# PEER gates through DRAM in three sets of 64 tokens in place of one set of 128

## The chip, the cores and the metric

One core of one Trainium2 chip. The metric is the time of the program on the device in microseconds (us), a median over runs.

## What is computed

A trunk of two layers on 256 tokens of width 1024: a short gated convolution (layer 0) or latent attention (layer 1), and after each a PEER channel mixer. The mixer picks, for every token and each of 8 heads, 16 of 16,384 experts, and sums their outputs:

```python
q = (xc @ w_q).reshape(C, PEER_HEADS, 2, PEER_HALF)
s = jnp.einsum("chpd,hpnd->chpn", q, subkeys)
top_s, top_i = lax.top_k(s, PEER_TOPK)
cand = top_s[:, :, 0, :, None] + top_s[:, :, 1, None, :]
best_s, best_pos = lax.top_k(cand.reshape(C, PEER_HEADS, PEER_TOPK * PEER_TOPK), PEER_TOPK)
ia = jnp.take_along_axis(top_i[:, :, 0], best_pos // PEER_TOPK, axis=-1)
ib = jnp.take_along_axis(top_i[:, :, 1], best_pos % PEER_TOPK, axis=-1)
expert = ia * PEER_KEYS + ib
g = jax.nn.softmax(best_s, axis=-1)
act = jax.nn.gelu(jnp.einsum("chkd,cd->chk", u_tab[expert], xc), approximate=False) * g
return jnp.einsum("chk,chkd->cd", act, v_tab[expert])
```

## The kernel before

The kernel does not gather experts. It multiplies all 16,384 u rows with all 256 tokens, takes the gelu, weighs it with a dense grid of gates (zero where an expert was not chosen), and multiplies the result with all v rows. The first key number `ia` has 128 values, which are worked through in four quarters of 32. One panel is the 128 experts of one `ia`: 128 x 1024 f32, 512 KB. A panel is loaded by SP into one of four buffers (`raw`), split by ACT into a rounded high part (`split_hi`, line 1012, four buffers) and by DVE into the remainder (`split_lo`, line 1414, two buffers); POOL splits panels in the stages before, but not in the mix. PE uses both parts. SP may load panel i when the low part of panel i-4 is made (semaphore `panel_lo_ready`).

The stages of one layer's PEER part are `sel` (the choice of the experts), `ahead` (26 u panels, j = 0 to 25), `mix` (three times 64 panels; `mix_body(q, it)`, q = 0 to 2, it = 0 to 7, does 4 u panels for quarter q+1 and 4 v panels for quarter q, u and v in turn), and `last` (32 v panels). The panels of one q are counted here from 0 to 63; panel 40 is the first u panel of `it` 5, panel 41 the v panel behind it. ACT's order around them is `split_hi(40)`, `split_hi(41)`, gelu of panel 36, copy of panel 38's bank, copies of gates, and `split_weighted`, whose result PE needs for panel 41.

The dense gates of a quarter (128 x 32 x 256 f32, in `arena`) must be there before that quarter is weighed. They are made in two ways:

- by matmul: a block is 16 tokens. DVE makes one-hot rows (`hot_b`, `hot_a`, `hot_g`, lines 1631 to 1640), PE multiplies them (`scatter` in the ahead stage, line 704; `scatter_side` in the mix, line 692), ACT and DVE copy the result to `arena` (lines 1083 and 1650). Quarter 1 of the four is made in ahead (16 blocks); in the mix, an `it` run with `by_matmul` makes two blocks of the next quarter.
- by DRAM: for tokens 0 to 127, POOL adds each chosen gate to a grid in DRAM with indirect transfers (`add_gates_by_dma`, line 1389): one transfer for each of the 128 (head, rank) pairs of a layer, 128 gates in each. After the 16 transfers of a head, POOL waits until they have all landed. ACT zeroes the grid (line 1092), and SP reads it into `arena` (`load_grid`, line 422): 8 loads of 4 first keys for each of the last two quarters.

So an `it` with `by_matmul` false is lighter for PE, ACT and DVE. Here all 8 `it` of q = 0 run by matmul; in q = 1 and 2, `it` 0 to 3 are light, and SP issues the grid loads ahead of the panels of `it` 5, 6 and 7 (3, 3 and 2 loads), behind a wait for the last transfer.

PE runs in program order. Its stream is written by hand, as are those of the other engines.

Of the kernel before, what the change touches and what calls it, by code (L numbers as in the profile page):

```python
# [60 lines left out]
BACK = 15  # L61
FIRST = KEYS // 8
BLOCKS = 48
NTH = {0: 16, 1: 24, 2: 32}
BY_GRID = 4
# [50 lines left out]
def program(nc, xT_in, c_in, pos_in, vec_in, con_in, ada_in, pan_in, key_in, iota_in, u_in, v_in, out):  # L116
    ctx = ExitStack()
    grid = [nc.dram_tensor(f"gates_by_expert{l}", (KEYS * KEYS * P, 1), F32, kind="Internal").ap() for l in range(2)]
    with ctx:
# [80 lines left out]
        place = sb("place", [P, SEL], I32)  # L200
        tok = sb("tok", [P, 1])
# [16 lines left out]
        row_start = arena[:, 12032:12032 + SEL]  # L218
        kept = g32_t[:, 0:SEL]
# [20 lines left out]
        GB = ps[6:8]  # L240
        BC = (SC[0], SC[1], STAT, SC[0], SC[1])
# [33 lines left out]
        start_ready = sem("row_starts_ready")  # L275
# [3 lines left out]
        added = [sem(f"gates_of_head{h}_added") for h in range(HEADS)]  # L279
# [97 lines left out]
        def _(sp):  # L377
# [16 lines left out]
            def load_experts(l):  # L394
# [23 lines left out]
                def load_grid(quarter, n):  # L418

                    a = quarter * QUART + 4 * n  # L420
                    to = arena[:, (quarter % 2 * QUART + 4 * n) * T:(quarter % 2 * QUART + 4 * n + 4) * T]
                    sp.dma_start(to.rearrange("p (a t) -> p a t", t=T)[:, :, 0:P],
                                 grid[l][a * KEYS * P:(a + 4) * KEYS * P].rearrange("(a p t) o -> p a (t o)", p=P, t=P)
                                 ).then_inc(s_grid, 16)

                with sp.Fori(0, 8) as it:
                    mix_loads(0, it)
                for q in (1, 2):
                    with sp.Fori(0, BY_GRID) as it:
                        mix_loads(q, it)  # L430
                    mix_loads(q, BY_GRID)
                    if q == 1:
                        sp.wait_ge(added[HEADS - 1], 16 * TOPK * (l + 1))
                    sp.wait_ge(w_mul, 64 * l + 16 * q)
                    for g, parts in enumerate(((0, 1, 2), (3, 4, 5), (6, 7))):
                        for n in parts:
                            load_grid(q + 1, n)
                        mix_loads(q, BY_GRID + 1 + g)
# [57 lines left out]
        def _(pe):  # L496
# [211 lines left out]
            def peer(l):  # L708
# [34 lines left out]
                def turn_back():  # L743

                    pe.wait_ge(idx_copied, TT * (l + 1))
                    for n, numbers in enumerate((ia_t, ib_t)):
                        by_rank = numbers[:, 0:P * DUP].rearrange("p (t r) -> p t r", r=DUP)[:, :, 0]
                        mm = pe.matmul(SC[0][:, n * P:(n + 1) * P], by_rank, ident_b[:], start=True, stop=True)
                    mm.then_inc(back_done, 1)

                for j in range(AHEAD - EARLY):
                    if j in TURN:
                        turn(TURN.index(j))
                    if j == BACK:
                        turn_back()
# [5 lines left out]
                pe.wait_ge(place_ready, l + 1)  # L761
# [13 lines left out]
                with pe.Fori(0, 8) as it:  # L775
                    mix_body(0, it, True)
                for q in (1, 2):
                    with pe.Fori(0, BY_GRID) as it:
# [227 lines left out]
        def _(act):  # L1006
# [84 lines left out]
            def peer(l):  # L1091
                nc.scalar.dma_start(grid[l][2 * QUART * KEYS * P:KEYS * KEYS * P].rearrange("(p c t) o -> p c (t o)", p=P, t=P),
                                    zero[:].bitcast(F32).unsqueeze(1).broadcast_to([P, 2 * QUART, P])).then_inc(s_zero, 16)
# [27 lines left out]
                def row_starts():  # L1121

                    act.wait_ge(tokens_ready, 1)
                    act.wait_ge(back_done, l + 1)
                    nc.scalar.activation(row_start, SC[0][:, P:2 * P], ACT.Identity, bias=tok[:], scale=float(P)
                                         ).then_inc(start_ready, 1)
                    nc.scalar.mul(kept, gate[:, 0, :], G_SCALE).then_inc(gates_kept, 1)
# [79 lines left out]
            act.sem_inc(g_read, 2)  # L1207
            act.wait_ge(s_c, 16)
# [143 lines left out]
        def _(pool):  # L1352
# [17 lines left out]
            pool.iota(tok[:], [[P, 1]], 0, 1, allow_small_or_imprecise_dtypes=True).then_inc(tokens_ready, 1)  # L1370
# [11 lines left out]
            def add_gates_by_dma(l):  # L1382

                pool.wait_ge(s_zero, 16 * (l + 1))
                pool.wait_ge(place_ready, l + 1)
                pool.wait_ge(gates_kept, l + 1)
                for h in range(HEADS):
                    for n in range(h * TOPK, (h + 1) * TOPK):
                        pool.indirect_dma_start(grid[l], bass.IndirectOffsetOnAxis(place[:, n:n + 1], 0), kept[:, n:n + 1], None,  # L1389
# [747 lines left out]
```

## Time and profile before

| | |
|---|---|
| median of 3 runs | 1887.38 us (1886.09 to 1890.06) |
| profiled execution, its own time | 1886.6 us |
| span in its profile | 1884.8 us |
| granted TensorE clock, mean | 0.992 of full speed |
| PE busy | 1866.2 us (99%) |
| DVE busy | 1492.7 us (79%) |
| ACT busy | 1001.2 us (53%) |
| POOL busy | 783.3 us (42%) |
| memory traffic, mean | 206 GB/s |

The profiled execution lies 0.8 us below the median. Of its time 1.8 us lie outside the span. A row of a timeline gives the start in us from the span's start, the duration in us, engine, line, operation and operands; brackets at its end give the idle time before it and who ended it. Layer 0's mix begins at about 301 us of the span, layer 1's at about 1243 us.

### The profile page before, as it was taken

To read this page: it belongs to the slowest core of one execution; us is meant where nothing else is said; L and a number is where in the kernel's file an instruction comes from. 1 tells how busy PE (TensorE), PEld (TensorE's weight loads), DVE (VectorE), ACT (ScalarE), POOL (GpSimd) and SP (SyncE) were. 2 spreads that over 40 slices of the span, in tenths; PEclk is the share of its full clock that TensorE was granted. 3 is DMA by queue.
4 is the path that set the end of the run, shared out by engine and by line. 5 is a ranking of instruction groups with operands and counts; after the bars stand their busy time and mean duration, and the time that the engine had idled before them with its cause. 6 is when DMAs were issued, how large, how long until landed. Compare 5 with 4: busy or idle time off the path is not lost.

```text
span 1884.8 us, 37910 instructions
## 1 busy us (share of the span) xinstructions
PE 1866.2 (99%) x12642; PEld 1655.2 (88%) x12642; DVE 1492.7 (79%) x2893; ACT 1001.2 (53%) x1598; POOL 783.3 (42%) x378
## 2 busy tenths in 40 slices
PE   8999999999999999999999999999999999999999
PEld 7999998888888888887789999988888888888887
DVE  6758999999778977997765489988887678668866
ACT  4354555555555555554454645555555555555553
POOL 3877548788860000000062575487888820000000
PEclk8999999999999999999998999999999999999999
DMA  9986657898897777876632565577777776667664
GB/s 352 364 271 202 187 136 185 229 225 230 229 244 245 257 233 236 264 233 225 223 114 83 170 200 168 136 159 182 184 179 189 190 215 194 187 193 215 190 191 140
DMA packets 174340, 388.82 MB, mean 206 GB/s; under 512 B 48801, under 2 KB 84001, under 8 KB 173857
## 3 DMA queue, kind: packets, MB, share of 16 engines
q1 hardware_dynamic: 120960, 379.01, 64.0%
q0 software_dynamic: 36864, 0.15, 4.7%
q10 hardware_dynamic: 16416, 8.39, 1.6%
q8 instruction: 56, 0.92, 0.2%
q14 instruction: 44, 0.35, 0.1%
HBM read 377.92 MB, written 9.57 MB: 206 GB/s over the span
## 4 chain that ended last, share of the span: by engine, by line
PE 92%; DVE 4%; DMA 2%; ACT 1%; issue 1%; POOL 1%; DVEq 0%; SPq 0%; ACTq 0%; POOLq 0%
PE bank L673 36%; PE bank L658 18%; PE bank L663 9%; PE bank L637 6%; PE bank L642 6%; PE bank L638 6%; PE bank L692 2%; PE bank L704 1%; DMA raw<-in_v_panels 1%; PE bank L720 1%; PE bank L522 1%; PE bank L502 1%; PE bank L953 1%; PE bank L504 1%; PE bank L503 1%
## 5 line engine op out<-in xcount | busy, mean ns | idle before, releaser
L1012 ACT CAST w_hi<-raw 128x1024 fp32r<-128x1024 f32 (+1 forms) x603 | 630.5, 1046 | 327.9 <-PE bank L673 104.0
L1414 DVE TENSOR_TENSOR w_lo<-raw,w_hi 128x1024 fp32r<-128x1024 f32 x488 | 596.9, 1223 | 192.4 <-PE bank L673 88.5
L1389 POOL DMA_INDIRECT gates_by_expert<-g_t,place x256 | 504.9, 1972 | 190.0 <-DVE place L1713 76.4
L1361 POOL TENSOR_TENSOR w_lo<-raw,w_hi 128x1024 fp32r<-128x1024 f32 (+2 forms) x115 | 273.3, 2380 | 528.3 <-PE bank L673 381.4
L658 PE MATMUL bank<-act_two,w_hi 128*128 128x512 f32 x1536 | 379.3, 389 | 0.0
L658 PEld LDWEIGHTS bank<-act_two,w_hi 128*128 128x128 f32 x1536 | 288.3, 188 | 59.8
L673 PE MATMUL bank<-w_hi,wt_hi 128*128 128x512 f32 x1024 | 325.5, 398 | 1.9 <-DVE wt_lo L1676 1.2
L673 PE MATMUL bank<-w_lo,wt_hi 128*128 128x512 f32 x1024 | 317.9, 391 | 0.0
L673 PE MATMUL bank<-w_hi,wt_lo 128*128 128x512 f32 x1024 | 317.0, 390 | 0.0
L637 PE MATMUL bank<-act_two,w_hi 128*128 128x256 f32 x984 | 246.1, 288 | 0.0
L638 PE MATMUL bank<-act_two,w_hi 128*128 128x256 f32 x984 | 241.2, 283 | 0.0
L673 PEld LDWEIGHTS bank<-w_hi,wt_lo 128*128 128x128 f32 x1024 | 192.3, 188 | 41.9
L673 PEld LDWEIGHTS bank<-w_lo,wt_hi 128*128 128x128 f32 x1024 | 192.2, 188 | 41.8
L663 PEld LDWEIGHTS bank<-act_two,w_lo 128*128 128x128 f32 x1536 | 209.5, 190 | 15.0
L663 PE MATMUL bank<-act_two,w_lo 128*128 128x256 f32 x1536 | 213.9, 282 | 0.0
L673 PEld LDWEIGHTS bank<-w_hi,wt_hi 128*128 128x128 f32 x1024 | 178.1, 189 | 32.0 <-issue 4.2
L1065 ACT COPY ring_g<-bank 128x256 f32 (+1 forms) x192 | 71.7, 374 | 253.1 <-PE bank L663 245.1
L638 PEld LDWEIGHTS bank<-act_two,w_hi 128*128 128x128 f32 x984 | 188.5, 192 | 0.0
L637 PEld LDWEIGHTS bank<-act_two,w_hi 128*128 128x128 f32 x984 | 188.2, 191 | 0.0
L642 PE MATMUL bank<-act_two,w_lo 128*128 128x256 f32 x984 | 138.5, 283 | 0.0
L642 PEld LDWEIGHTS bank<-act_two,w_lo 128*128 128x128 f32 x984 | 127.2, 192 | 0.0
L1631 DVE TENSOR_TENSOR hot_b<-ib_t,iota 128x2048 bf16<-128x2048 bf16 x96 | 116.9, 1218 | 0.8 <-PE bank L704 0.8
(257 smaller groups left out, 1951.2 us busy)
## 6 DMA issues: line engine op xcount, KB each, us to landing
raw<-in_u_panels SPq DMA_DIRECT2D x256, 512.0 KB
raw<-in_v_panels SPq DMA_DIRECT2D x256, 512.0 KB
raw<-in_panels SPq DMA_DIRECT2D x81, 512.0 KB
ada<-in_ada_rows SPq DMA_DIRECT2D x56, 512.0 KB
arena<-in_ada_rows SPq DMA_DIRECT2D x40, 512.0 KB, 7.0
gates_by_expert<-zero ACTq DMA_DIRECT2D x2, 4096.0 KB, 22.2
arena<-gates_by_expert SPq DMA_DIRECT2D x32, 256.0 KB, 5.3
gates_by_expert<-g_t,place POOLq DMA_INDIRECT x256
```

The source lines that it names most:

```text
L637: pe.matmul(bank, w_hi[:, hi_slot, w], acts[0][k], start=(k == 0), stop=False)
L638: pe.matmul(bank, w_hi[:, hi_slot, w], acts[1][k], start=False, stop=False)
L642: mm = pe.matmul(bank, w_lo[:, lo_slot, w], acts[0][k], start=False, stop=(k == KB - 1))
L658: pe.matmul(bank[:, 0:2 * T], w_hi[:, hi_slot, w], act_two[:, :, a], start=(k == 0), stop=False, skip_group_check=True)
L663: mm = pe.matmul(bank[:, 0:T], w_lo[:, lo_slot, w], act_hi[:, a], start=False, stop=(k == KB - 1), skip_group_check=True)
L673: mm = pe.matmul(YB[2 * t + n][:], wt[:, par, a], (w_hi, w_lo)[v][:, slots[v], n * 512:(n + 1) * 512], start=False, stop=False, skip_group ...
L1012: nc.scalar.copy(w_hi[:, slot, 0:width], raw[:, slot, 0:width]).then_inc(hi_done, 1)
L1065: nc.scalar.copy(ring_g[:, bass.ds(slot * T, T)], bank[:, T:2 * T]).then_inc(lo_copied, 1)
L1361: pool.tensor_tensor(w_lo[:, lo_slot, 0:width], raw[:, slot, 0:width], w_hi[:, slot, 0:width].bitcast(F32), ALU.subtract).then_inc(lo_done, 1)
L1389: pool.indirect_dma_start(grid[l], bass.IndirectOffsetOnAxis(place[:, n:n + 1], 0), kept[:, n:n + 1], None, compute_op=ALU.add).then_inc(a ...
L1414: dve.tensor_tensor(w_lo[:, lo_slot, 0:width], raw[:, slot, 0:width], w_hi[:, slot, 0:width].bitcast(F32), ALU.subtract).then_inc(lo_done, 1)
L1631: dve.tensor_tensor(wide(hot_b[:, par, :]), each(ib_t, KEYS, token0), numbers(0, KEYS), ALU.is_equal)
```

## The change

The tokens that go through DRAM become three sets of 64: set 0 (tokens 0 to 63) for quarters two to four, set 1 (64 to 127) for quarters three and four, set 2 (128 to 191) for the last quarter. One transfer now holds two ranks of a head for 64 tokens (128 gates again), so a set takes 64 transfers and a layer 192 in place of 128. POOL waits after the 8 transfers of a head and set. The light `it` are 0 and 1 in q = 0, 0 to 3 in q = 1, and 0 to 5 in q = 2: 12 in place of 8 in a layer. The grid is laid out by second key first, and set 2 has a grid of its own. Numbers and gates of a set are turned back by six small matmuls on PE, in ahead at j = 12 (sets 0 and 1) and at j = 15 (set 2). The cut diff:

```diff
-BACK = 15
+BACK = {12: (0, 1), 15: (2,)}
-BLOCKS = 48
-NTH = {0: 16, 1: 24, 2: 32}
-BY_GRID = 4
+SET = 64
+SETS = 3
+BLOCKS = 40
+BY_GRID = (2, 4, 6)
+FETCH_FROM = (5, 6, 5)
...
-                with sp.Fori(0, 8) as it:
-                    mix_loads(0, it)
-                for q in (1, 2):
-                    with sp.Fori(0, BY_GRID) as it:
+                for q in range(3):
+                    first = FETCH_FROM[q]
+                    with sp.Fori(0, first) as it:
                         mix_loads(q, it)
-                    mix_loads(q, BY_GRID)
-                    if q == 1:
-                        sp.wait_ge(added[HEADS - 1], 16 * TOPK * (l + 1))
-                    sp.wait_ge(w_mul, 64 * l + 16 * q)
-                    for g, parts in enumerate(((0, 1, 2), (3, 4, 5), (6, 7))):
-                        for n in parts:
+                    sp.wait_ge(added[q], 16 * SET * (l + 1))
+                    if q:
+                        sp.wait_ge(w_mul, 64 * l + 16 * q)
+                    for it in range(first, 8):
+                        for n in range((it - first) * 8 // (8 - first), (it - first + 1) * 8 // (8 - first)):
                             load_grid(q + 1, n)
-                        mix_loads(q, BY_GRID + 1 + g)
+                        mix_loads(q, it)
...
+                sp.dma_start(to[:, :, 0:tokens], by_key(grid0[l], P)[:, :, 0:tokens]).then_inc(s_grid, 16)
+                    if quarter == 3:
+                        sp.dma_start(to[:, :, P:P + SET], by_key(grid1[l], SET)).then_inc(s_grid, 16)
...
+                for n, grid, w, q in ((0, grid0, P, 1), (1, grid1, SET, 3)):
+                    to = grid[l].rearrange("(p n) o -> p (n o)", p=P)[:, q * QUART * w:KEYS * w]
...
+                for g in range(SETS):
+                    grid = (grid0, grid0, grid1)[g][l]
+                    pool.wait_ge(place_ready, SETS * l + g + 1)
+                    pool.wait_ge(gates_kept, SETS * l + g + 1)
+                    for h in range(HEADS):
+                        for n in range(g * SET + h * TOPK // 2, g * SET + (h + 1) * TOPK // 2):
+                            pool.indirect_dma_start(grid, bass.IndirectOffsetOnAxis(place[:, n:n + 1], 0), kept[:, n:n + 1], None,
+                                                    compute_op=ALU.add).then_inc(added[g], 16)
+                        pool.wait_ge(added[g], 16 * SET * l + 16 * TOPK // 2 * (h + 1))
...
+                def places(g):
+
+                    dve.wait_ge(gates_kept, SETS * l + g + 1)
...
+                for g in BACK[12]:
+                    places(g)
```

SP's queue in q = 0 of layer 0, at the end of `it` 4; before (`raw` are the panel buffers, `ada` a row of modulation weights):

```order
L382 DMA raw<-in_v_panels 128x1024
L406 REGISTER_ALU
L407 ISA [waits ada1_used]
L407 DMA ada<-in_ada_rows 128x1024
L426 REGISTER_ALU
L426 COMPARE_AND_BRANCH
```

and now:

```order
L387 DMA raw<-in_v_panels 128x1024
L411 REGISTER_ALU
L412 ISA [waits ada1_used]
L412 DMA ada<-in_ada_rows 128x1024
L435 REGISTER_ALU
L435 COMPARE_AND_BRANCH
L429 DMA arena<-gates_of_tile_0 128x4x64 [waits gates_of_set0_added]
L429 DMA arena<-gates_of_tile_0 128x4x64
L387 DMA raw<-in_u_panels 128x1024 [waits panel_lo_ready]
L387 DMA raw<-in_v_panels 128x1024 [waits panel_lo_ready]
```

Before, SP loops from `it` 4 straight to the panels of `it` 5. Now the load of panel 40, the first u panel of `it` 5, stands behind a wait for all 64 transfers of set 0 and behind two grid loads.

PE in the ahead stage between panel 11 and panel 12; before, the turn back stood between panels 14 and 15 (`g_t` holds the gates, `ia_t` and `ib_t` the key numbers):

```order
L704 MATMUL bank<-hot_g,hot_b 128x32 [waits gates_copied,one_hots_ready,chosen_experts_repeated]
L704 MATMUL bank<-hot_g,hot_b 128x32 x31
L748 MATMUL bank<-ident_b,ia_t 128x128 [waits chosen_experts_repeated]
L748 MATMUL bank<-ident_b,ib_t 128x128
L637 MATMUL bank<-act_two,w_hi 128x256 [waits panel_hi_ready,bank_read0]
```

and now, between panels 11 and 12:

```order
L647 MATMUL bank<-act_two,w_lo 128x256 x7
L756 MATMUL bank<-ident_b,ia_t 64x64 [waits chosen_experts_repeated]
L756 MATMUL bank<-ident_b,ia_t 64x64
L756 MATMUL bank<-ident_b,ib_t 64x64 x2
L759 MATMUL bank<-con,g_t 64x64 x2
L756 MATMUL bank<-ident_b,ia_t 64x64 [waits chosen_experts_repeated]
L756 MATMUL bank<-ident_b,ia_t 64x64
L756 MATMUL bank<-ident_b,ib_t 64x64 x2
L759 MATMUL bank<-con,g_t 64x64 x2
L642 MATMUL bank<-act_two,w_hi 128x256 [waits panel_hi_ready,bank_read0]
```

Twelve small matmuls now stand ahead of panel 12, and six more ahead of panel 15, where two stood; the numbers of sets 0 and 1 can reach POOL three panels sooner.

## Rows read from the trace of the kernel before

**Rows 1.** The page of the kernel before, part 1: engine, busy time and share.
```profile
PE 1866.2 (99%) x12642; PEld 1655.2 (88%) x12642; DVE 1492.7 (79%) x2893; ACT 1001.2 (53%) x1598; POOL 783.3 (42%) x378
```

**Rows 2.** Timeline of ACT, line L1070: start, duration, engine, line, operation.
```profile
1435.24 0.41 ACT L1070 ACTIVATE ring_g<-ring_g  x1
...
1523.46 0.41 ACT L1070 ACTIVATE ring_g<-ring_g  x1
...
1616.15 0.41 ACT L1070 ACTIVATE ring_g<-ring_g  x1
```

**Rows 3.** Timeline of POOL; in brackets idle time before and what ended it.
```profile
259.28 1.87 POOL L1389 DMA_INDIRECT gates_by_expert<-g_t,place  x1 [38.51 <-DVE place L1713]
...
407.96 2.30 POOL L1389 DMA_INDIRECT gates_by_expert<-g_t,place  x1 [2.70 <-DMA gates_by_expert<-g_t,place]
...
483.81 2.50 POOL L1389 DMA_INDIRECT gates_by_expert<-g_t,place  x1 [2.71 <-DMA gates_by_expert<-g_t,place]
...
523.11 2.59 POOL L1389 DMA_INDIRECT gates_by_expert<-g_t,place  x1 [3.53 <-DMA gates_by_expert<-g_t,place]
...
1200.60 1.82 POOL L1389 DMA_INDIRECT gates_by_expert<-g_t,place  x1 [37.89 <-DVE place L1713]
...
1431.76 2.42 POOL L1389 DMA_INDIRECT gates_by_expert<-g_t,place  x1 [3.14 <-DMA gates_by_expert<-g_t,place]
...
1478.33 1.55 POOL L1389 DMA_INDIRECT gates_by_expert<-g_t,place  x1 [2.81 <-DMA gates_by_expert<-g_t,place]
...
1497.88 2.46 POOL L1389 DMA_INDIRECT gates_by_expert<-g_t,place  x1 [0.30 <-issue]
```

**Rows 4.** Timeline of DVE where the one-hots of each layer begin.
```profile
247.33 1.22 DVE L1631 TENSOR_TENSOR hot_b<-ib_t,iota 128x2048 bf16<-128x2048 bf16 x1
...
258.15 0.28 DVE L1713 SCALAR_TENSOR_TENSOR place<-bank,arena 128x128 int32<-128x128 f32 x1
...
1188.75 1.22 DVE L1631 TENSOR_TENSOR hot_b<-ib_t,iota 128x2048 bf16<-128x2048 bf16 x1
```

**Rows 5.** Timeline of PE at the start of the first quarter, both layers.
```profile
300.92 1.30 PE L658 MATMUL bank<-act_two,w_hi 128*128 128x512 f32 x5
...
1242.79 1.53 PE L658 MATMUL bank<-act_two,w_hi 128*128 128x512 f32 x6
```

**Rows 6.** Timeline of SP's DMA queue: load of panel 40, both layers.
```profile
405.17 0.33 SPq L382 DMA_DIRECT2D raw<-in_u_panels  x1
...
1345.77 0.33 SPq L382 DMA_DIRECT2D raw<-in_u_panels  x1
```

**Rows 7.** Timeline of ACT and of PE at panels 40 and 41.
```profile
1350.80 1.05 ACT L1012 CAST w_hi<-raw 128x1024 fp32r<-128x1024 f32 x1
...
420.25 0.63 PE L673 MATMUL bank<-w_hi,wt_hi 128*128 128x512 f32 x2
...
1361.82 0.40 PE L673 MATMUL bank<-w_hi,wt_hi 128*128 128x512 f32 x1
```

**Rows 8.** Groups by line: busy us, mean ns of one, idle before.
```profile
L1414 DVE TENSOR_TENSOR w_lo<-raw,w_hi 128x1024 fp32r<-128x1024 f32 x488 | 596.9, 1223 | 192.4 <-PE bank L673 88.5 <-PE bank L663 80.1 <-issue 13.4
...
L1680 DVE TENSOR_TENSOR wt_lo<-w,wt_hi 128x512 fp32r<-128x512 f32 x122 | 83.2, 682 | 1.8 <-ACT wt_hi L1089 1.8
...
L1089 ACT CAST wt_hi<-w 128x512 fp32r<-128x512 f32 x122 | 76.5, 627 | 39.0 <-DVE w L1665 37.8 <-issue 0.6
...
L798 PE MATMUL bank<-con,arena 128*128 128x128 f32 x32 | 4.4, 276 | 1.2 <-DVE arena L1784 0.6 <-ACT arena L1197 0.6
```

**Rows 9.** Timeline of ACT and SP's queue where the grid is read.
```profile
1532.84 1.06 ACT L1012 CAST w_hi<-raw 128x1024 fp32r<-128x1024 f32 x1 [1.03 <-DMA raw<-in_u_panels]
...
593.41 1.05 ACT L1012 CAST w_hi<-raw 128x1024 fp32r<-128x1024 f32 x1 [3.17 <-DMA raw<-in_u_panels]
...
1705.03 2.58 SPq L422 DMA_DIRECT2D arena<-gates_by_expert  x3
```

**Rows 10.** The page, part 6: issues, KB each, us to landing.
```profile
gates_by_expert<-zero ACTq DMA_DIRECT2D x2, 4096.0 KB, 22.2
```

More of the change, by code:

```diff
@@ L117, in program @@
     ctx = ExitStack()
-    grid = [nc.dram_tensor(f"gates_by_expert{l}", (KEYS * KEYS * P, 1), F32, kind="Internal").ap() for l in range(2)]
+    grid0 = [nc.dram_tensor(f"gates_of_tile0_{l}", (KEYS * KEYS * P, 1), F32, kind="Internal").ap() for l in range(2)]
+    grid1 = [nc.dram_tensor(f"gates_of_tile1_{l}", (KEYS * KEYS * SET, 1), F32, kind="Internal").ap() for l in range(2)]
     with ctx:
@@ L199, in program @@
         lat = act32[:, 512:512 + 5 * T]
-        place = sb("place", [P, SEL], I32)
-        tok = sb("tok", [P, 1])
+        place = sb("place", [P, SETS * SET], I32)
+        tok = sb("tok", [P, 3])
         smax = sb("smax", [P, 3, 2])
@@ L278, in program @@
         s_zero = sem("gate_grid_zeroed")
-        added = [sem(f"gates_of_head{h}_added") for h in range(HEADS)]
+        added = [sem(f"gates_of_set{g}_added") for g in range(SETS)]
         s_grid = sem("gates_from_grid_landed")
@@ L773, in mix_body @@
                             v_panel(f"mix{l}", j + 3, 8, it, s, 1)
[L775 to L778, printed above, removed]
+                for q in range(3):
+                    with pe.Fori(0, BY_GRID[q]) as it:
                         mix_body(q, it, False)
-                    with pe.Fori(BY_GRID, 8) as it:
+                    with pe.Fori(BY_GRID[q], 8) as it:
                         mix_body(q, it, True)
@@ L1119, in turned, with row_starts @@
                     i.then_inc(gates_spread, 1)
-                def row_starts():
+                def row_starts(g):
                     act.wait_ge(tokens_ready, 1)
[L1124 to L1127, printed above, removed]
+                    act.wait_ge(back_done, SETS * l + g + 1)
+                    bank, c = BACK_BANK[g], slice(g * SET, (g + 1) * SET)
+                    for e in range(2):
+                        p = slice(e * SET, (e + 1) * SET)
+                        col = 1 - e + g % 2
+                        i = nc.scalar.activation(row_start[p, c], bank[p, SET:2 * SET], ACT.Identity,
+                                                 bias=tok[p, col:col + 1], scale=float(KEYS * (P if g < 2 else SET)))
+                    if g == 2:
+                        act.wait_ge(gate_parts, TT * (l + 1))
+                    nc.scalar.copy(kept[:, c], bank[:, 2 * SET:3 * SET]).then_inc(gates_kept, 1)
                 for j in range(AHEAD - EARLY):
@@ L1207, in _ @@
             act.sem_inc(g_read, 2)
+            act.sem_inc(g_first, FIRST)
             act.wait_ge(s_c, 16)
@@ L1382, in add_gates_by_dma @@
             def add_gates_by_dma(l):
[L1384 to L1389, printed above, removed]
-                                                compute_op=ALU.add).then_inc(added[h], 16)
-                    pool.wait_ge(added[h], 16 * TOPK * (l + 1))
+                pool.wait_ge(s_zero, 32 * (l + 1))
+                for g in range(SETS):
[7 more added lines that the diff above has]
+                        pool.wait_ge(added[g], 16 * SET * l + 16 * TOPK // 2 * (h + 1))
             select_panels(0)
@@ L1710, in experts @@
                         gate_part(l, 1)
-                    if j == BACK:
-                        dve.wait_ge(start_ready, l + 1)
-                        dve.scalar_tensor_tensor(out=place[:], in0=SC[0][:, 0:P], scalar=float(KEYS * P), in1=row_start,
-                                                 op0=ALU.mult, op1=ALU.add).then_inc(place_ready, 1)
+                    for g in BACK.get(j, ()):
+                        places(g)
                 weigh(0, 0, BLOCKS * l + 16 + 2)
```

76 lines of the change are left out of this document (43 added, 33 removed).

## Prediction

> **What bounds the kernel now.** I read the page's busy times first: PE is busy 99% of the span, and DVE, the next, 79% [rows 1]. So what PE no longer executes is a gain, unless something that was in time before comes late. Second I read what a light and a heavy `it` of the mix cost. Line 1070, the gelu of a summed bank, runs four times in each `it`, and its rows at the start of q = 1, of its `it` 4 and of q = 2 in layer 1 stand at 1435.24, 1523.46 and 1616.15 [rows 2]. Four light `it` take 88.22 us, 22.06 each; four heavy ones 92.69, 23.17 each. Third I read the three clocks that the change couples: POOL's transfers [rows 3], the start of the one-hots that follow the choice [rows 4], and the moment at which SP issues panel 40 of q = 0 and PE needs its neighbour [rows 5 to 7].
>
> **Removed: eight heavy `it`.** In each layer `it` 0 and 1 of q = 0 and `it` 4 and 5 of q = 2 become light. 8 x 1.12 = **-8.9 us**. DVE and ACT lose their part too, which lies under PE.
>
> **Added on PE: the turning back.** 18 small matmuls in a layer in place of two. Twelve are bf16, six f32. The nearest row is line 798, f32 of 128 columns: 4.4 us for 32, 0.14 each [rows 8]. The new ones have 64 columns. I take 0.14 for the six and half of it for the twelve bf16: 1.7 a layer, less 0.2 for the two that go, so 1.5. Below, it is near 0.6 a layer if a 64-column one takes half; above, 2.4 if all take 0.14. Two layers: **+3.0 us** (1.2 to 4.8). ACT's six instructions for sets 0 and 1 make the first one-hots wait about 1 us, but PE comes to the scatter behind them 0.9 us later as well; I take no stall.
>
> **Added: SP waits for set 0.** This is the term that decides, and it has three parts.
>
> When does set 0 start? DVE can write its places when the choice is done, where it now begins with the one-hots: 247.33 and 1188.75 [rows 4]. Before, the places were written at 258.15 and the first transfer began at 259.28, 1.13 later [rows 3, 4]. The same 1.1 here gives 248.6 and 1189.9, with the places themselves held back by nothing more.
>
> How long do 64 transfers take? In layer 1, six heads of 16 take 1431.76 - 1200.60 = 231.2 us, 38.5 each, wait included; in layer 0, four take 407.96 - 259.28 = 148.7, 37.2 each [rows 3]. Now POOL waits after 8. The waits before were 2.70 and 3.14 in these rows against 0.30 between two transfers, and I take 2.3 (layer 1) and 3.0 (layer 0) for each added one. Eight transfers then take (38.5 + 2.3)/2 = 20.4 and (37.2 + 3.0)/2 = 20.1. Beside light `it` POOL is slower: in layer 1 one head takes 1478.33 - 1431.76 = 46.6, and the 8 transfers behind a wait 1497.88 - 1478.33 = 19.55, which with a wait more is about 22.1; in layer 0 a head takes 523.11 - 483.81 = 39.3, so 8 take 21.05 with the added wait [rows 3]. Layer 1: the mix starts at 1242.8 [rows 5], by when 52.9/20.4 = 2.6 groups of the 8 are done; the two light `it`, 44.1 us, do 2.0; the other 3.4 take 69.6. Set 0 is in the grid at 1242.8 + 44.1 + 69.6 = **1356.5**. Layer 0: 2.6 by 300.9, 2.1 in the light ones, 3.3 x 20.1 = 66.3: **411.3**.
>
> Who waits? SP came to panel 40 at 1345.77 and 405.17 [rows 6], so it is late by some 11 and 6 us (and its own 0.7 earlier arrival). Behind it stand panels 40 to 43; PE still has 36 to 39. After set 0: two grid issues, 1.0 us (three took 2.58 [rows 9], which would make it 1.7); panel 40 lands in at most 5.0 us, since ACT took it 5.03 after its issue without a wait on DMA [rows 6, 7], and I take 4.4; `split_hi(40)` 1.05; `split_hi(41)`, which lands right behind, 1.3; a gelu of 0.41 [rows 2] and a copy, taken as long; the copies of gates, 0.6; `wt_hi` 0.63; on DVE `wt_lo` 0.68 and `split_lo(41)` 1.22 [rows 8]; semaphores 0.3. Together 12.0 us from set 0 to PE's panel 41. PE began panel 41 at 1361.82 and 420.25 [rows 7]; two light `it` and the turning back move that by -2.2 + 1.5 = -0.7. Set 0 is thus in time up to 1349.1 and 407.5. PE's stall is 1356.5 - 1349.1 = 7.4 in layer 1 and 411.3 - 407.5 = 3.8 in layer 0: **+11.2 us**. The buffers behind refill faster than PE empties them, so the stall comes once a layer.
>
> Sets 1 and 2 are in time by the same rates. In layer 1 set 1 ends near 1525, and SP comes to it at about 1557; set 2 ends near 1695, while SP's grid loads now stand at 1705 to 1707.6 [rows 9] and move on by some 6.
>
> One rule of the Trainium skill is weighed here. The rows say that POOL issues slower beside light `it`, 46.6 us a head against 38.5. "SBUF — State Buffer" (section Who interferes with whom) says that a DVE instruction with two SBUF inputs contends with a GpSimd one that reads SBUF. By that, fewer one-hots on DVE would free POOL, and set 0 would be no slower in the light `it`; the stall of layer 1 would be 3.9, and the sum lower by 3.5. The measured rows decide for me, since they are of this very pairing.
>
> **More grid loads.** The 16 loads of the grid in a layer become 32: q = 0 gets 8 of 64 tokens, q = 1 has its 8 in two bursts of four, and q = 2 has 16 in bursts of 4, 6 and 6 in place of 3, 3 and 2. Behind a burst of three ACT waited 1.03 us for the panel in layer 1 and 3.17 in layer 0 [rows 9], and PE did not stall. For six the two ends are nothing and, at double the wait over two bursts, about 6 us in layer 0. ACT's lead covers most of it: **+1.0 us** (0 to 6). "DMA: Bandwidth & Descriptors" (Specifications) wants 512 B for line rate, and a row of 64 tokens is 256 B; no row here has such a load, and my bound counts it as a whole load already.
>
> **Zeroing.** The zeroes grow from 4.2 to 7.3 MB a layer. The 4096 KB landed in 22.2 us [rows 10], so these need some 39. ACT issues them ahead of all 22 panels of `sel` and of 12 of `ahead`, so they are in time for the first transfer. Panels share the memory with them there for 17 us more; nothing up to 3 us, and I take 0.
>
> **Sum**, against the profiled execution's 1886.6: -8.9 + 3.0 + 11.2 + 1.0 = +6.3, 1892.9. The median of the runs lies 0.8 higher, so **1893.7 us**, 0.3% slower. Less than 0.2% (3.8 us) either way is what a measurement of this kernel can hardly tell from no change.
>
> **Rivals.**
> 1. *Set 0 is late by only a little.* If the light `it` do not slow POOL, layer 1's set takes 8 x 20.4 = 163.2, ends at 1353.1 and costs 4.0; with layer 0 at 248.6 + 160.8 = 409.4, 1.9. Sum -8.9 + 3.0 + 5.9 + 1.0 = +1.0: 1888.4, no change. For it: waits after every 8 break the pace into which POOL fell; against it: that pace is in the rows. 0.23.
> 2. *Set 0 is in time, the change is faster.* It needs 64 transfers in 159 us, 19.9 for each 8, or 4 to 7 us more slack in the chain of 12. Layer 0's 20.1 is within 1% of that, layer 1's 20.4 within 3%, so a wait that costs less than its predecessors would do where no light `it` slow POOL. Then -8.9 + 3.0 + 0 to 1: 1881.5 to 1882.5. It decides when set 0 ends before 1349 and 407. 0.27.
> 3. *The bursts of q = 2 stall PE too* and set 0 is as above: up to 6 more, 1900. It is within the likeliest case's sign; 0.1 of its 0.50.
>
> The likeliest, a stall in both layers, has 0.50 and its own range 1891.3 to 1901. Faster by over 0.2% 0.27, within 0.2% 0.23, slower by over 0.2% 0.50. The range that holds it 8 times in 10 takes in most of the rivals: 1880 to 1901.
>
> **What would show it.** In the changed kernel's trace: the first transfer of each layer near 248.6 and 1190, SP's first grid load of q = 0 near 411 and 1357 rather than at 404 and 1345, ACT's wait for panel 40 on DMA, and a gap on PE at panel 41 of 2 to 10 us in each layer; light `it` of 22.06 us; no gap at `it` 6 of q = 1. Without the gaps the term of set 0 is wrong: either POOL was quicker than 20 us for 8, or the chain of 12 us is shorter than I made it. With gaps elsewhere, above all at `it` 6 and 7 of q = 2, the bursts were priced too low.

## The result: 3.2% slower, and the profile after

| | before | changed |
|---|---|---|
| median, us | 1886.75 (1886.09 to 1890.06, 4 runs) | 1947.18 (1945.86 to 1950.8, 4 runs) |
| ratio, 95% interval | | 1.032 [1.0301, 1.0338] |
| profiled execution, us | 1886.6 | 1950.8 |
| its span, mean granted clock | 1884.8, 0.992 | 1949.0, 0.980 |

The prediction said 1893.7, within 1880 to 1901. The sign came out, the size did not: 60 us were lost where 6 were forecast.

The busy line of the page of the changed kernel, which answers to [rows 1]:

```profile
PE 1867.7 (96%) x12430; PEld 1653.7 (85%) x12430; DVE 1450.8 (74%) x2801; ACT 994.5 (51%) x1580; POOL 1027.2 (53%) x506
```

The page counts 212 matmuls fewer than before, and PE is busy for as long as before (1866.2 there). The rest of the span, 1949.0 - 1867.7 = 81.3 us, is idle, where before had 18.6. So the loss is PE standing still, 62.7 us more of it. The view of waits, PE alone (engine, line, releaser: us in total, times, longest), says for what:

```profile
PE bank L616 <- DVE ring_g L1467: 42.3, 3, 21.1
PE bank L663 <- ACT w_hi L1023: 11.7, 2, 7.1
PE bank L678 <- DVE w_lo L1436: 9.8, 10, 2.3
```

Line 616 spreads the inverse norm at the start of `peer`, a place of which the prediction said nothing. DVE's `ring_g` is only the last link. The timeline of ACT shows the first; ACTq is the part of ACT that issues DMAs:

```profile
130.48 22.29 ACTq L1106 DMA_DIRECT2D gates_of_tile<-zero  x2
152.81 0.26 ACT L1042 ACTIVATE ring_g<-bank,eps 128x2 f32<-128x2 f32 x1 [21.93 <-issue]
...
1106.67 22.65 ACTq L1106 DMA_DIRECT2D gates_of_tile<-zero  x2
1129.37 0.26 ACT L1042 ACTIVATE ring_g<-bank,eps 128x2 f32<-128x2 f32 x1 [22.28 <-issue]
```

`peer` begins with two zeroing DMAs in place of one: 6144 KB for the first grid, 1024 KB for the second. Issuing the pair took 22.3 and 22.6 us. The view of the tile (duration in ns: least, median, greatest) shows that one of the two issues takes it all:

```profile
L1106 ACTq DMA_DIRECT2D gates_of_tile<-zero x4: 387/11125/22227, 130.5 to 1107.1; - x4
```

An issue of 0.4 us and one of 22.2. ACT's next instruction, the square root of the norm, is queued behind, and PE waits for the norm. PE's timeline and its windows (us busy and matmuls, granted clock, DMA share, GB/s):

```profile
153.33 1.22 PE L616 MATMUL bank<-con,ring_g 128*128 128x128 f32 x4 [20.70 <-DVE ring_g L1467]
...
1129.88 1.22 PE L616 MATMUL bank<-con,ring_g 128*128 128x128 f32 x4 [21.07 <-DVE ring_g L1467]
```

```profile
110.00:130.00 20.00, 19.21 (x158) 1.00 0.67 228
130.00:150.00 20.00, 2.44 (x14) 0.66 1.03 301
150.00:155.00 5.00, 1.67 (x6) 0.50 1.04 288
155.00:160.00 5.00, 5.00 (x33) 0.81 0.65 185
160.00:170.00 10.00, 10.00 (x85) 1.00 0.41 115
```

PE stands still for 20.7 and 21.1 us, and as it resumes the granted clock is at the lower level, 0.50 of full speed or 1.2 GHz; it is back at 2.4 by 160. The idle time is 41.8 us, and the slow matmuls behind come on top.

The second group, lines 663 and 678, is mostly the term on which the prediction rested. POOL's timeline, the first transfer of each layer, which answers to [rows 3]:

```profile
270.55 2.41 POOL L1411 DMA_INDIRECT gates_of_tile<-g_t,place  x1 [27.61 <-DVE place L1726]
...
1246.45 2.37 POOL L1411 DMA_INDIRECT gates_of_tile<-g_t,place  x1 [27.02 <-DVE place L1726]
```

SP's timeline, its first grid loads of each layer, and the row of the view of SP's waits for them:

```profile
437.67 0.94 SPq L429 DMA_DIRECT2D arena<-gates_of_tile  x2
...
1415.75 0.93 SPq L429 DMA_DIRECT2D arena<-gates_of_tile  x2
```

```profile
SPq L429 <- DMA gates_of_tile<-g_t,place: 27.7, 2, 15.6
```

And PE's timeline behind them:

```profile
444.17 3.41 PE L663 MATMUL bank<-act_two,w_hi 128*128 128x512 f32 x8 [4.54 <-ACT w_hi L1023]
450.41 1.22 PE L678 MATMUL bank<-w_hi,wt_hi 128*128 128x512 f32 x2 [1.88 <-DVE w_lo L1436]
...
1422.89 2.49 PE L663 MATMUL bank<-act_two,w_hi 128*128 128x512 f32 x5 [7.14 <-ACT w_hi L1023]
...
1428.00 0.72 PE L678 MATMUL bank<-w_hi,wt_hi 128*128 128x512 f32 x2 [0.33 <-DVE w_lo L1436]
```

Line 663 multiplies u panels and line 678 v panels, so the first and third rows are panel 40 and the other two panel 41. Set 0 takes 437.67 - 270.55 = 167.1 us and 169.3, and SP waits twice, 27.7 us together. PE stalls for 4.5 us ahead of panel 40 and 1.9 ahead of panel 41 in layer 0, and for 7.1 and 0.3 us in layer 1.

**The ledger.** Idle: 41.8 (zeroing) + 13.5 (set 0) + about 7 in gaps of 0.5 to 2.3 us (first passes of q = 0, grid loads in q = 1 and 2 of layer 0) = 62. Busy: the light passes and the turning back should have taken 8.9 - 2.4 = 6.5 off; it is 1.5 above before instead, so by this estimate about 8 us went into slower clocks behind the gaps. e5 below has the same matmuls, no gap over 2.7 us and PE busy for 1857.6, 10.1 less.

### The profile page after: what moved, and what is told of

Read it like the earlier page. It is cut to its first block, busy times and chain, and to the rows that moved or that the text cites. A ratio compares the mean times of both kernels' runs of the same rounds, so it can differ in the third digit from the quotient of the medians.

```text
span 1949.0 us, 37267 instructions
## 1 busy us (share of the span) xinstructions
PE 1867.7 (96%) x12430; PEld 1653.7 (85%) x12430; DVE 1450.8 (74%) x2801; ACT 994.5 (51%) x1580; POOL 1027.2 (53%) x506
## 4 chain that ended last, share of the span: by engine, by line
PE 67%; POOL 12%; DMA 7%; DVE 5%; issue 3%; ACTq 2%; ACT 1%; DVEq 1%; SPq 0%; POOLq 0%
PE bank L678 28%; PE bank L663 13%; POOL gates_of_tile L1411 11%; PE bank L668 7%; DMA gates_of_tile<-g_t,place 4%; PE bank L642 4%; PE bank L647 4%; PE bank L643 4%; ACTq L1106 2%; DMA raw<-in_u_panels 1%; DMA raw<-in_panels 1%; DVE w_lo L1436 1%; DMA raw<-in_v_panels 1%; POOL w_lo L1381 1%; PE bank L697 1%
## 5 line engine op out<-in xcount | busy, mean ns | idle before, releaser
L1411 POOL DMA_INDIRECT gates_of_tile<-g_t,place x384 | 749.4, 1951 | 308.5 <-DMA gates_of_tile<-g_t,place 136.5
L1687 DVE TENSOR_TENSOR w<-ring_g,arena 128x512 f32 (+1 forms) x122 | 84.5, 693 | 34.5 <-issue 29.8
## 6 DMA issues: line engine op xcount, KB each, us to landing
gates_of_tile<-zero ACTq DMA_DIRECT2D x2, 6144.0 KB, 25.3
```

Source lines behind the costliest of these rows:

```text
L1411: pool.indirect_dma_start(grid, bass.IndirectOffsetOnAxis(place[:, n:n + 1], 0), kept[:, n:n + 1], None, compute_op=ALU.add).then_inc(adde ...
L1687: dve.tensor_tensor(w32[:], ring_g[:, bass.ds(slot * T, 2 * T)], arena[:, bass.ds(key * T, 2 * T)], ALU.mult).then_inc(w_mul, 1)
```

## The experiments

Ratios are to the kernel before on the same chip, whose medians were 1882.8 to 1885.4 us there.

### The second zeroing DMA

**e1.** The first grid is still zeroed at the start of `peer`, the second one later, at panel 5 of `ahead` (the edit is cut at `...`, here and below):

```
...
+                zero_grid(grid0, P, 1)
...
                     if j == EXP_AFTER:
+                        zero_grid(grid1, SET, 3)
                         act.wait_ge(gate_in, l + 1)
```

> The changed kernel with ACT's second zeroing (the 1 MB grid of set 2) moved from right behind the first to panel 5 of the ahead stage. Theory A: ACT is held for 22 us in each layer by issuing a second DMA on its queue behind the first, and with it PE (gaps of 20.7 and 21.1 us); expected 1947.2 - 42 for the gaps and some 2 more for the lower clock behind them, about 1903 us, no gap on PE there. Theory B: it is the bytes of the zeroes and the later sets that cost, and PE would stall elsewhere at the start of the layer: over 1930 us.

1901.83 us (1899.77 to 1908.4), 1.0088 [1.0068, 1.0108]. Both issues are short now. ACT's timeline:

```profile
128.53 0.39 ACTq L1105 DMA_DIRECT2D gates_of_tile<-zero  x1
...
223.03 0.37 ACTq L1105 DMA_DIRECT2D gates_of_tile<-zero  x1
```

The gaps at line 616 are gone, the stalls behind set 0 remain (4.4 + 1.8 and 2.8 + 2.0 us). From 1.032 to 1.0088 is 2.3%, some 44 us: the same bytes by the same queue, only not back to back.

**e3.** The kernel before, its 4 MB of zeroes cut in two equal DMAs:

```
-                nc.scalar.dma_start(grid[l][2 * QUART * KEYS * P:KEYS * KEYS * P].rearrange("(p c t) o -> p c (t o)", p=P, t=P),
-                                    zero[:].bitcast(F32).unsqueeze(1).broadcast_to([P, 2 * QUART, P])).then_inc(s_zero, 16)
+                for a, n in ((2 * QUART, QUART), (3 * QUART, QUART)):
+                    nc.scalar.dma_start(grid[l][a * KEYS * P:(a + n) * KEYS * P].rearrange("(p c t) o -> p c (t o)", p=P, t=P),
+                                        zero[:].bitcast(F32).unsqueeze(1).broadcast_to([P, n, P])).then_inc(s_zero, 16)
```

> The kernel before, with its one zeroing of 4 MB made as two of 2 MB back to back on ACT's queue, same bytes. Theory A in its wide form (any second DMA waits until the first is nearly done): ACT is held some 10 us in each layer, 1887 + 16 to 22, about 1905 us. Narrow form (a limit on what the queue holds, above 4 MB or 8192 rows of 512 B): no change, 1887.

1901.03 us (1896.61 to 1907.58), 1.0079 [1.0057, 1.0102], by one more instruction a layer: the wide form of the theory. **e6.** The changed kernel with its two zeroing DMAs in the other order, 1 MB first:

```
-                for n, grid, w, q in ((0, grid0, P, 1), (1, grid1, SET, 3)):
+                for n, grid, w, q in ((1, grid1, SET, 3), (0, grid0, P, 1)):
```

> The changed kernel with the order of ACT's two zeroing DMAs swapped: the 1 MB one first, the 6 MB one behind it; same bytes, same place, same queue. Theory 1 (the second issue is held until the first one's descriptors have gone, so the hold goes with the size of the first): the first takes 3 to 6 us, so the second issue holds ACT about 3.5 to 5 us instead of 22.3, PE's gaps at its first panels of peer go from 21 to 2 to 4 us, the clock dips less, and the time falls from 1947 to 1906 to 1915. Rival (the second is held by its own size, or two DMAs of ACT's always cost the sum of both): ACT is held 20 us or more, 1945 or more. Rival 2 (the hold is gone but set 0's start stays tied to the zeroing's end, so the stall at set 0 remains as in e1): this only adds to theory 1, gaps of 3 to 7 us near 416 and 1380.

1911.82 us (1907.26 to 1913.87), 1.0138 [1.0119, 1.0156], as theory 1 had it. **e9.** The kernel before, cut into 4032 KB and 64 KB behind them:

```
-                nc.scalar.dma_start(grid[l][2 * QUART * KEYS * P:KEYS * KEYS * P].rearrange("(p c t) o -> p c (t o)", p=P, t=P),
-                                    zero[:].bitcast(F32).unsqueeze(1).broadcast_to([P, 2 * QUART, P])).then_inc(s_zero, 16)
+                for a, n in ((0, 2 * QUART - 1), (2 * QUART - 1, 1)):
+                    to = grid[l][2 * QUART * KEYS * P:KEYS * KEYS * P].rearrange("(p c t) o -> p c (t o)", p=P, t=P)[:, a:a + n]
+                    nc.scalar.dma_start(to, zero[:].bitcast(F32).unsqueeze(1).broadcast_to([P, n, P])).then_inc(s_zero, 16)
```

> The kernel before with its 4 MB zeroing DMA cut in two unequal ones, issued back to back by ACT: 4032 KB, and 64 KB behind it. Same bytes. It tells what the second issue waits for. Theory (the issue is held until what stands ahead of it on the queue has mostly gone, whatever its own size): by 22.2 us behind 6 MB and 8.3 to 8.9 behind 2 MB, ACT is held 15 us (13 to 17) each time, PE has a gap of 13 to 15 us at its first matmul of peer in each layer, and the time is 30 us (26 to 38) over before. Rival (the issue waits only for room for its own rows): 64 KB fits at once, ACT is held under 2 us, PE has no gap over 1.5 us, and the time is that of before within 4 us.

1912.58 us, one run, 29 us above the median of before (1883.5), as the theory had it. ACT's pairs of issues in the timelines of e3, e6 and e9, in this order:

```profile
129.95 8.29 ACTq L1093 DMA_DIRECT2D gates_by_expert<-zero  x2
1083.91 8.91 ACTq L1093 DMA_DIRECT2D gates_by_expert<-zero  x2
```

```profile
130.88 3.79 ACTq L1106 DMA_DIRECT2D gates_of_tile<-zero  x2
1089.17 3.66 ACTq L1106 DMA_DIRECT2D gates_of_tile<-zero  x2
```

```profile
129.59 14.72 ACTq L1094 DMA_DIRECT2D gates_by_expert<-zero  x2
1083.10 14.54 ACTq L1094 DMA_DIRECT2D gates_by_expert<-zero  x2
```

| first, then second | pair of issues, us | us for a MB of the first |
|---|---|---|
| 1 MB, 6 MB (e6) | 3.7, 3.8 | 3.7 |
| 2 MB, 2 MB (e3) | 8.3, 8.9 | 4.3 |
| 3.94 MB, 64 KB (e9) | 14.5, 14.7 | 3.7 |
| 6 MB, 1 MB (changed) | 22.3, 22.6 | 3.7 |

The second issue is held for a time that goes with the size of the first and not with its own: 64 KB behind 4 MB is held 14 us, 6 MB behind 1 MB less than 4. The rival, that an issue waits for room for its own rows only, is out. All four have PE's gaps at the same place, 2.1, 7, 13 and 21 us. e7 below issues the 6 MB alone: 0.4 us, and no gap at this place. What in the queue is full until then, no run shows (every zeroing DMA here writes rows of 512 B), nor whether a second DMA on another engine's queue would be held.

### When SP waits for a set

**e4** moves SP's wait for set 0 by one pass, and nothing else:

```
-FETCH_FROM = (5, 6, 5)
+FETCH_FROM = (6, 6, 5)
```

> The changed kernel with only SP's fetch moved to it 6. If the late set 0 and the zeroing are separate costs: 14 us below the changed kernel, about 1933. If the set is late mainly because the whole layer started 21 us late: no change, 1947.

1936.7 us (1927.71 to 1942.63), 1.0287 [1.0262, 1.0312]. The gaps at panels 40 and 41 are gone, those at line 616 stay (20.6 and 20.6), and one of 1.9 us shows up behind set 2. So the two costs are separate, as the first theory had it. The ratio fell by only 0.3%, though, 6 us where 14 were expected, with 15 us between the fastest and the slowest of the four runs. **e2** is the same on top of e1:

> As e1, and SP fetches set 0's gates from it 6 of q = 0 on in place of it 5, so that its wait comes 23 us later. Theory A with the late set 0: the gaps of 6.4 and 7.1 us at panels 40 and 41 go, and with them up to 3 us more; expected about 1889 us, 14 below e1. Rival: the burst of four loads per it costs as much as the wait did, or the gaps come back at it 6: within 4 us of e1.

1893.33 us (1891.49 to 1898.35), 1.0047 [1.0031, 1.0062]. Set 0 is no longer waited for, and with that time gone another wait is laid bare. POOL's last transfer, SP's waits and PE:

```profile
1718.22 1.54 POOL L1413 DMA_INDIRECT gates_of_tile<-g_t,place  x1 [0.30 <-issue]
```

```profile
SPq L429 <- DMA gates_of_tile<-g_t,place: 15.0, 1, 15.0
```

```profile
1730.53 2.92 PE L663 MATMUL bank<-act_two,w_hi 128*128 128x512 f32 x6 [9.79 <-ACT w_hi L1023]
```

Set 2 of layer 1 comes 15 us after SP. In e1 and in the changed kernel SP had not waited for it. **e5** moves this wait too:

```
-FETCH_FROM = (6, 6, 5)
+FETCH_FROM = (6, 6, 6)
```

> The kernel of e2, with SP's wait for set 2 moved from it 5 to it 6 of q=2. Theory (three separate costs: ACT held by its second zeroing DMA, set 0 late, set 2 late once set 0's loads are moved): the gap of 9.8 us at 1720.8 in e2, which ended with a wait of 15 us of SP's for set 2, goes; no PE gap over 2 us is left, and the time is 1893.3 - 9.8 = about 1883.5 (1881 to 1887), the same as before. The eight heavy passes that became light are then paid back by the turning back (+1.2 a layer), a gap of 1.0 to 1.2 us at the first passes of q=0, and the denser grid loads. Rival A: six loads of the same bytes in two passes (16 DMAs with panels between) make bursts that stall PE, in both layers, for 3 us or more: 1888 or more. Rival B: the light passes pay in full and it beats before: 1879 or less.

1889.94 us (1886.01 to 1894.89, 10 runs), 1.0029 [1.0017, 1.0041]. The gap of 9.8 is gone, but the time isn't the expected 1883.5: rival A is right for layer 0, where PE has gaps of 2.7, 2.6 and 1.3 us at 807, 834 and 857 (before has the last one as well, 1.2), and wrong for layer 1, which has none there.

### The loads in a group

**e8** spreads layer 0's loads over three passes again:

```
-FETCH_FROM = (6, 6, 6)
+FETCH_FROM = ((6, 5, 5), (6, 6, 6))
...
-                    first = FETCH_FROM[q]
+                    first = FETCH_FROM[l][q]
```

> The kernel of e5 (zeroing apart), with SP's first pass of grid loads set by layer: it 6, 5, 5 in layer 0 and it 6, 6, 6 in layer 1. In e5 the sets of layer 0 had landed by 586 and 755 us, it 5 of q=1 and of q=2 begins at 587 and 769, so the loads can go over three passes instead of two there. Theory (what e5 lost were bursts of 24 grid loads in two passes of layer 0, where the modulation rows are fetched too: PE gaps of 2.6, 2.6 and 1.3 us at 807, 834 and 857): those gaps go back to under 1.5 each, the quarters of layer 0 take 541 to 542.5 us after the work ahead (548 in e5, 542 in e2), layer 1 stays at 538, and the time is e5's less 5: 1885 (1882 to 1887), against 1885.4 of before: the same or faster by up to 0.2%. Rival A: set 1 comes a few us after it 5 of q=1 in layer 0, SP waits, and PE stalls 2 us or more near 600: 1887 to 1890. Rival B: layer 0's lost time isn't the bursts but the lighter passes themselves (POOL's transfers beside PE's feeders): 1889 or more.

1889.58 us (1882.5 to 1899.46, 12 runs), 1.0032 [1.0012, 1.0052]: a miss. The number of passes wasn't it: the gaps are still 1.7, 2.5 and 1.2 us. Rival A is there in small: SP waits 4.0 us for set 1 of layer 0, and PE 1.2 us behind it. SP's timeline in `it` 7 of q = 2, then ACT's and PE's:

```profile
812.80 0.33 SPq L412 DMA_DIRECT2D ada<-in_ada_rows  x1
813.17 0.44 SPq L429 DMA_DIRECT2D arena<-gates_of_tile  x1
813.65 0.52 SPq L431 DMA_DIRECT2D arena<-gates_of_tile  x1
814.21 0.64 SPq L429 DMA_DIRECT2D arena<-gates_of_tile  x1
814.89 1.38 SPq L431 DMA_DIRECT2D arena<-gates_of_tile  x1
816.31 3.16 SPq L429 DMA_DIRECT2D arena<-gates_of_tile  x1
819.51 0.64 SPq L431 DMA_DIRECT2D arena<-gates_of_tile  x1
820.19 0.50 SPq L387 DMA_DIRECT2D raw<-in_u_panels  x1
```

```profile
826.23 1.05 ACT L1023 CAST w_hi<-raw 128x1024 fp32r<-128x1024 f32 x1 [7.18 <-DMA raw<-in_u_panels]
```

```profile
832.94 0.74 PE L678 MATMUL bank<-w_hi,wt_hi 128*128 128x512 f32 x2 [2.49 <-DVE w_lo L1438]
```

The six grid loads stand ahead of the panel; the fifth issue alone is held 3.2 us. The panel goes out 7.0 us after the first of them and its cast comes 6.0 us later still. **e10** changes only the place of the loads, one block of four keys ahead of each pair of panels:

```
-                def mix_loads(q, it):
+                def mix_loads(q, it, grids=()):
                     for e in range(4):
+                        for n in grids[e:e + 1]:
+                            load_grid(q + 1, n)
...
-                        for n in range((it - first) * 8 // (8 - first), (it - first + 1) * 8 // (8 - first)):
-                            load_grid(q + 1, n)
-                        mix_loads(q, it)
+                        mix_loads(q, it, range((it - first) * 8 // (8 - first), (it - first + 1) * 8 // (8 - first)))
```

> The kernel of e8 with SP's grid loads placed between the panel loads of a pass (one block of four keys ahead of each pair of panels) instead of in a group ahead of the pass. Same loads, same passes. In e8's trace the group of six issues at 813.2 to 820.1 stands ahead of the next panel; that panel's cast on ACT waited 7.2 us for its DMA and PE stood still for 2.5 us at 830.5. Theory (the group delays the panels behind it): PE's gaps at 602, 805, 830 and 854 (1.2, 1.7, 2.5, 1.2) fall to under 1 each, about 4 us in all, and the time is 1884 to 1886 where e8 had 1889.6, or within 0.2% of before. Rival A: the DMA engines as a whole are behind in these passes (share of 0.9 and more), so the same panels come late wherever the grid loads stand: the gaps stay, 1888 or more. Rival B: the spread around the mean clock, not the gaps, makes the medians: the trace shows the gaps gone, the median stays above before by 3 us or more.

**1881.38 us (1877.29 to 1886.3, 12 runs), 0.9988 [0.9977, 0.9998]**, better than forecast and the first version ahead of before. Of PE's gaps in layer 0's last passes only the one that before has as well is left (1.2 at 847). Windows of 795 to 860, e8's and then e10's:

```profile
795.00:860.00 65.00, 59.65 (x347) 1.00 0.75 244
```

```profile
795.00:860.00 65.00, 63.83 (x369) 1.00 0.79 249
```

The DMA engines do more in the same time, so it was order and not throughput (rival A out). A part isn't explained. PE's idle time in the traces falls by 5.4 us from e8 to e10 (26.1 and 20.7), the ratio by 0.44%, 8 us; four of e8's twelve runs had a mean clock of only 0.990, for which no run gives a cause. And the gaps of about 1 us at the first passes of q = 0, ahead of any grid load, are gone in e10 and in e11 as well.

**e12** asks whether before could have had this too: its own loads between its panels, nothing else.

> The kernel before with its grid loads placed between the panel loads of a pass, as in e10, and nothing else. It tells whether e10's 2.5 us under before come from the sets or from the placing, which before could have had as well. Theory (before has three small loads a pass in a group and loses 1.2 us at 849 and 0.5 elsewhere to it): it is within 0.1% of before, 1883 to 1885 where before has 1884, so the eight passes without scatter are what e10 gains by. Rival (the placing alone is worth 2 us or more): 0.999 of before or less, and the sets give nothing.

1884.71 us (1881.24 to 1888.2, 12 runs), 1.001 [0.9999, 1.002]: the placing alone gives before nothing, as expected. **e7** and **e11** leave out the third set (its tokens stay with PE's scatter, and there is one zeroing DMA), e7 with the loads in groups from `it` 6 on, e11 with the passes of e8 and the loads placed as in e10:

```
-BACK = {12: (0, 1), 15: (2,)}
+BACK = {12: (0, 1)}
...
-SETS = 3
+SETS = 2
...
-BY_GRID = (2, 4, 6)
+BY_GRID = (2, 4, 4)
...
```

> The changed kernel with sets 0 and 1 alone: tokens 128 to 191 stay with PE's scatter in q=2, the second grid and its zeroing DMA are gone, so ACT issues one zeroing DMA of 6 MB, and the grid loads begin in it 6 of each quarter. Passes without scatter are 10 a layer, against 8 before and 12 in the changed kernel. Theory: 2 passes a layer by 1.1 us = -4.5, turning back with 12 small matmuls for 2 (+0.8 a layer, +1.6), the gap of about 1.1 at the first passes of q=0 (+2.2): about 0.7 under before, that is the same: 1882 (1879 to 1886). Rival A (the second zeroing DMA is the only large cost): the 22 us holds of ACT are gone here as well, so this holds too; it differs only where set 0 late costs even from it 6. Rival B (the third set is what pays; without it the change costs): 1886 or more. Rival C: fewer transfers on POOL (256 a layer) mean less contention with PE's feeders, and it beats before: 1879 or less.

> The kernel of e7 (two sets, one zeroing DMA) with the grid loads between the panels as in e10 and the passes of e8 (it 6, 5, 5 in layer 0; 6, 6, 6 in layer 1). Passes without scatter: 10 a layer (8 before). Theory: e7 was at 1.001 of before; the small gaps that its trace still shows in layer 0 (0.6, 0.6 and 1.4 us) lose about 1 us, so 0.9995 to 1.0015 of before, that is the same. Rival A: the placing of the loads is worth 3 us or more here too: 0.9985 or less. Rival B: one placed behind a panel is issued too late for the first pass of the next quarter, DVE waits for the grid and PE gaps of 2 us or more open at the quarter's start: 1.003 or more.

e7: 1887.8 us (1884.16 to 1893.76, 12 runs), 1.001 [1.0, 1.0021], a small miss: 2 us above before where 0.7 below was expected. e11: 1882.72 us (1879.1 to 1889.01, 11 runs), 0.9992 [0.9979, 1.0004]. The placing and the passes of layer 0 together are worth about 0.2% here, and the two intervals overlap. e10 and e11 can't be told apart: what the third set adds is too small for these runs to show.

## Why the prediction was wrong, step by step

**The step that failed is the zeroing.** It read "nothing up to 3 us, I take 0". I costed the bytes (would they land in time, and what do they take from the panels) and was right on both, but the change also turns one issue on ACT's queue into two in a row, and I never priced the second issue or asked who is queued behind it. It cost 41.8 us of idle PE, and about 44 with the clock behind it (e1 against the changed kernel). One look at what ACT does right after [rows 10]'s DMA would have named the victim. No row of before could price it, since before has no second DMA behind a large one; the upper end should then have been the duration of the first. At the rate of [rows 10], 22.2 us for 4 MB, that is 33 us for 6 MB (e1's took 32.5) and 67 for two layers, so the range would have reached 1960 and held the 1947.

The zeroing is not the whole miss. Without it, in e1, the change costs 0.88%, 16.6 us, where the sum had 6.3. e1's trace has 15.5 us more idle PE than before: 10.9 behind set 0, where I had 11.2, and 4.6 elsewhere, mostly in gaps of 1 to 2 us at the first passes of q = 0 and behind grid loads, where I had 1.0. PE's busy time in that trace, at a mean clock of 0.987, is 6.3 us above before, so the gain of the light passes does not show.

**Set 0 late: the mechanism right, the size low.** Forecast were 3.8 and 7.4 us at panel 41. PE had done panel 39 by 439.6 and 1415.8, and panel 40 takes 2.8 us when nothing is in the way, so panel 41 was due at 442.4 and 1418.5. It began at 450.4 and 1428.0, that is 8.0 and 9.5 us late: 6.4 and 7.5 us of idle time, most of it ahead of panel 40, which waits for its own cast, and the rest slower matmuls of panel 40 behind the gap (the granted clock is 0.62 from 444 to 448).

The start was right: 270.55 - 21.9 (ACT's hold) = 248.65, forecast 248.6 (rows 3 and 4 add up to 248.5). The chain from set 0 to panel 41 was nearly right too: 12.7 and 12.3 us, forecast 12.0. Low was the time of the set, 167.1 and 169.3 us for 162.7 and 166.6. POOL's timeline where its fourth group of 8 transfers begins, in each layer:

```profile
327.92 1.96 POOL L1411 DMA_INDIRECT gates_of_tile<-g_t,place  x1 [3.01 <-DMA gates_of_tile<-g_t,place]
...
1303.78 2.20 POOL L1411 DMA_INDIRECT gates_of_tile<-g_t,place  x1 [2.84 <-DMA gates_of_tile<-g_t,place]
```

The first three groups took 57.4 and 57.3 us, 19.1 each, where I had 20.1 and 20.4. The five beside the mix took 21.9 and 22.4 each, where I had 20.5 and 21.1 on average: POOL was slower there beside heavy passes as well as beside light ones. The waits that I added (2.3 us in layer 1, 3.0 in layer 0) were not those of my rows either, which give 2.8 and 2.4. The stall of 3.9 us in layer 1 that the rule on shared ports (the Trainium skill, "SBUF — State Buffer", Who interferes with whom) would have given did not come; the row's 7.4 was nearer.

**Light passes: right.** The gelus at the start of `it` 0, 6 and 7 of q = 2 in layer 1, which answer to [rows 2]:

```profile
1682.46 0.41 ACT L1081 ACTIVATE ring_g<-ring_g  x1
...
1814.85 0.41 ACT L1081 ACTIVATE ring_g<-ring_g 128x256 f32<-128x256 f32 x1
...
1838.03 0.41 ACT L1081 ACTIVATE ring_g<-ring_g 128x256 f32<-128x256 f32 x1
```

Six light ones take 132.39, 22.07 each, the heavy one 23.18. Over the whole mix of layer 1 the same rows of before and of e10, the first and the last start:

```profile
1250.53 0.41 ACT L1070 ACTIVATE ring_g<-ring_g  x1
...
1773.96 0.41 ACT L1070 ACTIVATE ring_g<-ring_g 128x256 f32<-128x256 f32 x1
```

```profile
1249.51 0.41 ACT L1081 ACTIVATE ring_g<-ring_g  x1
...
1768.45 0.41 ACT L1081 ACTIVATE ring_g<-ring_g 128x256 f32<-128x256 f32 x1
```

523.4 us against 518.9: the four light passes of a layer give their 4.5 where nothing stands in their way.

**Turning back: 2.4 us for 3.0.** The time from one and the same matmul of the scores in `sel` (line 720, in the changed kernel 725) to the mix has the turning in it. Before and changed, layer 0:

```profile
182.86 0.68 PE L720 MATMUL bank<-arena,ring_g 128*128 128x128 f32 x4 [0.61 <-DVE arena L1502]
```

```profile
205.02 0.68 PE L725 MATMUL bank<-arena,ring_g 128*128 128x128 f32 x4 [0.61 <-DVE arena L1524]
...
324.32 1.98 PE L663 MATMUL bank<-act_two,w_hi 128*128 128x512 f32 x8
```

300.92 [rows 5] - 182.86 = 118.06, and 324.32 - 205.02 = 119.30: 1.2 a layer, where I took 1.5. In layer 1 the last matmul of this line begins at 1148.4 and 1205.1, 94.4 and 95.6 us ahead of the mix: 1.2 again.

**Sets 1 and 2 in time: right here, for the wrong reason.** SP did not wait for them in the changed kernel. In e2, where SP no longer waits for set 0, set 2 is there at 1721 and not at 1695: in layer 1 sets 1 and 2 take 182 and 177 us there, more than the 20.4 us for 8 transfers that I took. ACT's hold of 22 us did not help, since it moves POOL's start as much as PE's: e1 has no hold, and SP does not wait for set 2 either. Against e2, SP comes to that wait 7 us later in e1, counted from the start of the mix, and POOL needs 507 us from its first to its last transfer in place of 528. Why POOL is quicker there, no run shows.

**More grid loads: +1.0 was low** for the groups: about 5 us of new gaps in layer 0, inside the upper end of 6. The sign of it was in my own row of ACT's 3.17 us wait behind three loads [rows 9].

**The rivals.** The first two did not hold; of the third, the bursts, about 5 us came; none named the zeroing. Faster, by the light passes, is what only the mended kernel shows: with the zeroing apart, the waits one pass later where the sets come late, and the loads between the panels, e10 is 0.12% under before. Of the -8.9 + 2.4 = -6.5 us that this should give, the two medians show 2.5 (1881.4 and 1883.8) and the two profiled spans 5.4 (1879.4 and 1884.8); the rest stays open.

## What to carry to other kernels

A DMA that is added on an engine's queue has two prices, its bytes and its issue; where another of some MB has just gone out on the same queue, take the first one's whole duration as the upper end of the second issue's price and look up what that engine was to do next. Small loads that are inserted into a stream of prefetches go between them, one at a time: a group in front puts its whole length on the next prefetch, 7.0 us for six loads here. With three loads a pass, in the kernel before, the placing changed nothing. And after one late transfer is mended, look for the next: it may have been in time partly because of the stall.

## What the hardware showed that I had not expected

- The second of two DMA issues in a row on ACT's queue held ACT for 3.7 to 4.3 us for each MB of the first, whatever the second's own size (64 KB to 6 MB). The pair is issued 2 to 4 us before the first has landed: after 3.7, 14.6 and 22.4 us, with medians of 7.5, 16.9 and 25.3 us from issue to landing for the first of 1, 3.94 and 6 MB.
- The same two issues 95 us apart cost 0.4 us each (e1).
- Behind a gap of 21 us PE began again at the lower level of its clock (0.50 from 150 to 155). By the 0.81 from 155 to 160 it stayed there for some 3.5 us, an estimate.
- Single runs of one kernel differ with the mean granted clock: e8's fastest was 1882.5 us at 0.995, its slowest 1899.5 at 0.990. With 10 to 12 runs of a kernel, the intervals of the ratios are still 0.2 to 0.4% wide.
